# The same tiles in another order in the on-chip memory: bm, bmh, st and gbt declared elsewhere

## What is computed

```python
def hybrid_mixer(h, w_in, b_merge, conv_w, w_out_conv, w_out_attn, w_o):   # block one
    xc, bg, cg, zc, q, k, v, za, g_conv, g_attn = jnp.split(h @ w_in, splits, axis=-1)
    c = causal_depthwise_conv(cg * xc, conv_w)
    y_conv = (silu(zc) * bg * c) @ w_out_conv
    o = mixture_of_dilations(q, k, v, alibi_slopes(16))      # 16 heads of 64
    y_attn = (silu(za) * o) @ w_out_attn
    merged = sigmoid(g_conv + b1) * y_conv + sigmoid(g_attn + b2) * y_attn
    return merged @ w_o
...
for layer in range(2):                                       # block two
    # layer 0: compressed, selected and windowed attention; layer 1: block attention
    mix = jnp.concatenate([o_main, o_mem], -1) @ w_out       # o_mem: attention to 256 memory rows
    x = layer_norm(ALPHA * x + mix, ln1_g[layer], ln1_b[layer])
    ffn = (gelu(conv3(a)) * b) @ w_ffn_out                   # a, b = split(x @ w_ffn_in)
    x = layer_norm(ALPHA * x + ffn, ln2_g[layer], ln2_b[layer])
```

## Time and profile before

| | |
|---|---|
| median of 3 runs | 1009.47 us (1008.49 to 1012.89) |
| profiled execution, time / span | 1008.49 us / 1006.8 us |
| instructions | 20008 |
| busy: TensorE / VectorE / ScalarE / GpSimd | 951.1 / 667.0 / 525.9 / 130.4 us |
| mean granted TensorE clock | 0.989 of full speed |
| DMA | 172.89 MB, 172 GB/s over the span |

### The profile page before, as it was taken

One profiled execution on the slowest core, in us unless ns is written; L12 is line 12 of the kernel. 1 busy time (PEld: TensorE's weight loads), 2 busy tenths in 40 slices (PEclk: granted clock), 3 DMA queues, 4 the chain that ended last, 5 costly groups with the idle time before them and its releaser, 6 DMA issues.

```text
span 1006.8 us, 20008 instructions
## 1 busy us (share of the span) xinstructions
PE 951.1 (94%) x7010; PEld 861.1 (86%) x7018; DVE 667.0 (66%) x1204; ACT 525.9 (52%) x966; POOL 130.4 (13%) x154
## 2 busy tenths in 40 slices
PE   7999999999999888989799999998899989999995
PEld 5899999999899876757699999996788678999995
DVE  5566666666666857874866666668576576666666
ACT  5545555555444547654645555555466455555553
POOL 3000000000100402630600000006100060000001
PEclk9999999999999999999999999999999999999998
DMA  7555555556465475213365555553654346555552
GB/s 249 183 190 177 177 177 190 178 172 225 155 210 170 145 243 167 96 37 126 105 227 188 187 188 188 186 184 111 231 173 154 123 135 202 188 188 188 188 189 78
DMA packets 48226, 172.89 MB, mean 172 GB/s; under 512 B 6031, under 2 KB 6479, under 8 KB 48060
## 3 DMA queue, kind: packets, MB, share of 16 engines
q1 hardware_dynamic: 44732, 159.78, 48.0%
q0 software_dynamic: 3456, 12.61, 4.1%
HBM read 171.29 MB, written 1.07 MB: 171 GB/s over the span
## 4 chain that ended last, share of the span: by engine, by line
PE 79%; DVE 9%; ACT 5%; DMA 4%; issue 1%; POOL 1%; SPq 0%; POOLq 0%; ACTq 0%; DVEq 0%
PE bank L1318 17%; PE bank L1319 17%; PE bank L1320 17%; PE ysum L1366 6%; PE ysum L1368 6%; PE ysum L1367 6%; DVE sb_wl L806 4%; DMA sb_raw<-in_stream 4%; ACT sb_wh L417 2%; PE bank L1397 2%; PE ysum L1410 1%; PE ysum L1404 1%; ACT sb_xh L442 1%; DVE sb_z L852 1%; ACT sb_pr L462 1%
## 5 line engine op out<-in xcount | busy, mean ns | idle before, releaser
L806 DVE TENSOR_TENSOR sb_wl<-sb_raw,sb_wh 128x1024 fp32r<-128x1024 f32 x300 | 388.9, 1299 | 174.9 <-ACT sb_wh L417 173.6
L1318 PE MATMUL bank<-sb_xh,sb_wh 128*128 128x256 f32 x1360 | 384.1, 282 | 4.5 <-DVE sb_t_a L1230 2.5
L1319 PE MATMUL bank<-sb_xl,sb_wh 128*128 128x256 f32 x1360 | 380.6, 280 | 0.0
L1320 PE MATMUL bank<-sb_xh,sb_wl 128*128 128x256 f32 x1360 | 380.6, 280 | 0.0
L417 ACT ACTIVATE sb_wh<-sb_raw 128x1024 fp32r<-128x1024 f32 x300 | 314.5, 1053 | 120.3 <-PE ysum L1368 48.2
L1318 PEld LDWEIGHTS bank<-sb_xh,sb_wh 128*128 128x128 f32 x1360 | 257.0, 189 | 13.9 <-issue 5.6
L1320 PEld LDWEIGHTS bank<-sb_xh,sb_wl 128*128 128x128 f32 x1360 | 258.8, 190 | 0.0
L1319 PEld LDWEIGHTS bank<-sb_xl,sb_wh 128*128 128x128 f32 x1360 | 256.1, 188 | 1.5
L1366 PE MATMUL ysum<-sb_wh,sb_mh 128*128 128x512 f32 x208 | 81.7, 393 | 3.2 <-DVE sb_ml L816 3.2
L1367 PE MATMUL ysum<-sb_wl,sb_mh 128*128 128x512 f32 x208 | 81.7, 393 | 0.0
L1368 PE MATMUL ysum<-sb_wh,sb_ml 128*128 128x512 f32 x208 | 81.7, 393 | 0.0
(11 more groups left out here) (264 smaller groups left out, 1440.0 us busy)
## 6 DMA issues: line engine op xcount, KB each, us to landing
sb_raw<-in_stream SPq DMA_DIRECT2D x300, 512.0 KB, 3.3
sb_bias<-rel_rows POOLq DMA_DIRECT2D x12, 384.0 KB, 3.7
sb_bias<-in_alibi POOLq DMA_DIRECT2D x8, 256.0 KB, 3.1
sb_gb<-in_ln_g POOLq DMA_DIRECT2D x4, 512.0 KB, 4.1
sb_gb<-in_ln_b POOLq DMA_DIRECT2D x4, 512.0 KB, 6.7
sb_x_tok<-in_x SPq DMA_DIRECT2D x2, 512.0 KB, 3.8
sb_memf<-in_mem_t POOLq DMA_DIRECT2D x1, 1024.0 KB, 6.2
out<-sb_x_tok SPq DMA_DIRECT2D x2, 512.0 KB, 2.6
```

Of the source, the lines that this page charges most:

```text
L806: dve.tensor_tensor(wl[slot][:, :, :], raw[slot][:, :, :], wh[slot][:, :, :].bitcast(F32), ALU.subtract).then_inc(split_l, 1)
L1318: pe.matmul(out, wh[slot][:, k, :], mov_h(k), start=k == 0, stop=False)
L1319: pe.matmul(out, wh[slot][:, k, :], mov_l(k), start=False, stop=False)
L1320: last = pe.matmul(out, wl[slot][:, k, :], mov_h(k), start=False, stop=k == KT - 1)
```

## The change

Four small tiles are declared at another place. gbt goes from behind meml to behind gb; bm, bmh and st go from behind z to the end of the list, ahead of half. No instruction, wait, shape or loop is touched.

```diff
         z = sb("z", [P, NT, D])
-        bm = sb("bm", [P, 2, KT])
-        bmh = sb("bmh", [P, 2, KT])
-        st = sb("st", [P, 16])
         xh = sb("xh", [P, KT, T], F32R)
         xl = sb("xl", [P, KT, T], F32R)
         gb = sb("gb", [P, 2, D])
+        gbt = sb("gbt", [P, 10, KT])
         mixh = sb("mixh", [P, 2, KT, T], F32R)
...
         meml = sb("meml", [P, KT, T], F32R)
         qall = gates[:, 1]
-        gbt = sb("gbt", [P, 10, KT])
         mh = sb("mh", [P, 2, T], F32R)
...
         convf = sb("convf", [P, 2, FT, 4])
+        bm = sb("bm", [P, 2, KT])
+        bmh = sb("bmh", [P, 2, KT])
+        st = sb("st", [P, 16])
         half = sb("half", [P, 1])
```

## The result

The changed kernel takes 1023.86 us in the median of 4 runs (1021.62 to 1025.76), the one before 1008.98 (4 runs). The ratio is 1.0155, with a 95% interval of 1.0136 to 1.0176. I had forecast 1009.5 us within 1006.5 and 1014.0, with a chance of 0.045 for slower by more than 0.5%. The forecast was wrong.

A forecast was written before the change was run, and what follows sets the result against it. TensorE was taken to bound the kernel, busy 951 of 1006.8 us. The four parts summed 0 + 0 + 0 + 0, so the forecast stayed at the median of before, 1009.5 us, with a range of 1006.5 to 1014.0.

The forecast's parts named there:

- Part one: TensorE's matmuls and weight loads: operand starts modulo 128 do not set their pace; cost 0.
- Parts two, three and four: VectorE and ScalarE starts modulo 128; GpSimd's norm instructions on st; bm, bmh, gbt and transfers: cost 0 each.
- The bound of 9.8 us: Upper end for st: GpSimd's scaling and power at their slowest in five norms, 9.8 us.
- A: Faster: xh and xl at 0 modulo 128 give TensorE's quicker pace throughout; 12.0 us, so 997.5 us; chance 0.04.
- C: Slower within the bound: the shift tips stage one's quicker TensorE pace into the slower; 4.1 us, 1013.6 us; chance 0.04.
- B: Slower: GpSimd's single-element accesses to st slow when it straddles 64 bytes; up to 9.8 us, 1019.3 us; chance 0.03.
- D: Layout stays the same because tiles are not placed in declaration order; 1009.5 us; chance 0.86 together with the forecast.
- What would make it wrong: Shifts of 64 or 128 bytes change which accesses of different engines meet in the memory; no size given.

The follow-up runs named there:

- u4_before_all64: The kernel before with 64 unused bytes ahead of raw0, so every tile starts 64 bytes higher; 1010.03 us, ratio 1.0006 to before.
- u1_x_back: The change plus three unused tiles: xh, xl, gb at their old start, mixh to convf at theirs modulo 128; 1009.02 us, ratio 0.9989 to before.
- b1_placed: The change plus four unused tiles, setting distances to wh0 modulo 256 to xh 192, mixh 192, mh 32; 1005.52 us, ratio 0.9943 to before.

## Why the prediction was wrong

**Part one is the step that failed: "The address does not choose between them. Cost: 0."** By the steps in the table of the result, it cost 11.5 us on xh and xl and 3.5 us on the rows. My pairs of rows compared the start of one operand at a time. But in the wide product wh and wl move and xh stands, and in the others xh moves and wh stands, so all of them had the same pair of starts, 192 apart modulo 256. Both mixh and memh were 192 away as well. The rows could not tell the cases apart, because the trace of before held only one distance of a 256-column matmul on these tiles. That two paces occurred on one tile at one address was read correctly; that the address therefore plays no part did not follow. The distance decides which paces there are, and at 192 the work before decides between them.

**The modulus.** I went by 64 and 128. The one that counts for xh is 256, in which every tile that takes part moved against wh. Not every such move costs: mixh went from 192 to 64, and the mean step of its matmuls stayed at 117.8 ns.

**Parts two, three and four held.** VectorE, ScalarE and GpSimd were not touched by the new starts: 667.6 us for 667.0, 525.9 for 525.9, 130.6 for 130.4. The pair on st went from 193 and 558 ns to 196 and 559. The bound of 9.8 us for it was never drawn on.

**The rivals.** A had TensorE's pace on xh depend on the layout, which is right, but on the start of xh alone and with the wrong sign. In u4_before_all64 xh starts at 0 modulo 128 and keeps its two paces; at a distance of 0 modulo 256 there is a third pace, slower than both. C came nearest. It let the shift tip the quicker pace of stage one into the slower, 960 x 4.3 ns = 4.1 us. The quicker pace did go, but to 119.9 ns, and the slower pace of stage one, of the feed-forward and of the rows went up as well. Its term was mis-sized by the 10.9 us that lie between 4.1 and 15.0. It had 0.04. B fell with u1_x_back and b1_placed, and with the times of the instructions on st. D is refuted by the result.

**What would make it wrong** named tiles that collide in their new places, but as accesses of different engines. The runs point to two operands of the same engine.

**The rule on ports.** The Trainium skill, page "SBUF — State Buffer", section "Who interferes with whom", says that TensorE waits for no other engine, and lists two read ports for it, one for the moving operand and one for the loading of weights, as independent. The first half agrees with the runs: the whole difference between 113.3 and 120.0 ns is there with the other engines silent. The second does not: whether the step is 113.3 or 120.0 ns hangs on the distance between exactly these two operands, and here the measurement decides. That the two reads meet in the memory is my reading of it; the runs show the dependence on the distance, not the place where they meet.

## What to carry to other kernels

A reordering of tiles cost this kernel, which is bound by TensorE, 1.5% without an instruction being changed, and a placement picked by its measured steps won 0.5% over the kernel before. Where such matmuls follow each other without a gap, take the step from start to start, not the duration, and note the distance between the standing and the moving tile modulo 256 beside it. Compare with rows that differ in this distance, and if the trace has none, say that the cost is not bounded; a few bytes of unused tile are a cheap way to try.

## What the runs showed of the hardware

The step of a 128x256 matmul at a full clock, with weights loaded for each, takes one of several values, from 113.3 to 120.1 ns, set by the distance between its two operands modulo 256 bytes, in units no coarser than 32 bytes, and in part by the matmuls that went before. At a distance of 192 there are two such values, 113.5 and 117.8 ns; one of them holds through whole blocks (96 matmuls in stage one), and another product in between can switch it. A tile that is not an operand of these matmuls at all (mh) can in this way change their time by 4.3 ns each. It also works the other way: the place of xh changed the step of the 128x512 matmuls on mh from 226.7 to as much as 230.9 ns. What keeps this state was not found, nor was the curve measured between the multiples of 32 bytes.
